# A transformer block with a SwiGLU feed-forward: gate, up and down each as seven block products, in two phases

## The reference

```
D_MODEL = 2048; SEQ = 512; D_FF = 5632
def swiglu(h, wg, wu, wd):
    return (jax.nn.silu(h @ wg) * (h @ wu)) @ wd
...
h = rms_norm(x, norm_ffn_g[i])
x = x + swiglu(h, ffn_w_gate[i], ffn_w_up[i], ffn_w_down[i])
```

## Time and profile before

| | us |
|---|---|
| median of three runs | 2318.69 |
| lowest and highest of them | 2315.89, 2318.73 |
| the profiled execution | 2316.0 |
| its span, first to last instruction | 2314.1 |
| TensorE busy in it | 2288.2 (99%) |
| VectorE busy | 1305.3 (56%) |
| ScalarE busy | 777.7 (34%) |
| mean granted TensorE clock | 0.995 |

### The profile page before, as it was taken

The page is one execution under the profiler, slowest core; times in us unless marked ns, Lnnn a source line. Parts: engine busy times, 40 slices in busy tenths (PEclk is TensorE's granted clock), DMA queues, the critical chain, the costliest instruction groups (busy, mean ns, idle before and its releaser), DMA issues.

```text
span 2314.1 us, 30956 instructions
## 1 busy us (share of the span) xinstructions
PE 2288.2 (99%) x11963; PEld 1967.9 (85%) x11963; DVE 1305.3 (56%) x1993; ACT 777.7 (34%) x1163; POOL 76.2 (3%) x89
## 2 busy tenths in 40 slices
PE   8999999999999999999999999999999999999998
PEld 7898989889889999888888888888888888888886
DVE  5333466665765556456464646465565646464647
ACT  4332344443453334222332323232332323232322
POOL 1000000000010000000000000000000000000000
PEclk9999999999999999999999999999999999999999
DMA  5343211222123213355253544435343535253434
GB/s 162 115 118 87 79 52 50 65 64 64 56 82 111 74 59 97 95 168 147 92 154 92 155 119 125 140 109 150 115 137 110 145 99 151 91 151 119 128 109 137
DMA packets 225456, 252.81 MB, mean 109 GB/s; under 512 B 14172, under 2 KB 188273, under 8 KB 224161
## 3 DMA queue, kind: packets, MB, share of 16 engines
q1 hardware_dynamic: 218050, 222.36, 30.5%
q0 software_dynamic: 7264, 28.51, 6.4%
HBM read 223.55 MB, written 4.19 MB: 98 GB/s over the span
## 4 chain that ended last, share of the span: by engine, by line
PE 77%; issue 19%; DVE 2%; POOL 1%; ACT 1%; DMA 0%; POOLq 0%; SPq 0%; ACTq 0%; DVEq 0%
PE ps L1266 76%; POOL rqn L415 1%; DVE wl L759 0%; PE ps L1577 0%; DVE hTl L759 0%; DVE x_rows L773 0%; PE ps L1613 0%; PE ps L1313 0%; DVE x_rows L1187 0%; POOL krr L415 0%; DMA down<-in_ffn_w_down_dram 0%; DVE down L1162 0%; ACT wh L455 0%; ACT hTh L455 0%; ACT x_sq L472 0%
## 5 line engine op out<-in xcount | busy, mean ns | idle before, releaser
L1266 PE MATMUL ps<-hTh,wh 128*128 128x512 f32 (+1 forms) x1968 | 764.0, 388 | 2.4 <-DVE wl L759 1.8
L1266 PE MATMUL ps<-hTh,wl 128*128 128x512 f32 (+1 forms) x1968 | 760.1, 386 | 0.0
L1266 PE MATMUL ps<-hTl,wh 128*128 128x512 f32 (+1 forms) x1968 | 759.7, 386 | 0.0
L759 DVE TENSOR_TENSOR wl<-raw,wh 128x1024 fp32r<-128x1024 f32 x298 | 363.3, 1222 | 341.8 <-ACT wh L455 339.1
L455 ACT ACTIVATE wh<-raw 128x1024 fp32r<-128x1024 f32 x298 | 314.2, 1058 | 534.6 <-PE ps L1266 416.7
L1266 PEld LDWEIGHTS ps<-hTh,wh 128*128 128x128 f32 x1968 | 370.0, 188 | 75.2 <-issue 2.2
L1266 PEld LDWEIGHTS ps<-hTh,wl 128*128 128x128 f32 x1968 | 369.8, 188 | 75.1
L1266 PEld LDWEIGHTS ps<-hTl,wh 128*128 128x128 f32 x1968 | 370.0, 188 | 72.2
L759 DVE TENSOR_TENSOR wl<-down,wh 128x1024 fp32r<-128x1024 f32 x132 | 161.4, 1223 | 157.0 <-ACT wh L455 157.0
L1266 PE MATMUL ps<-wh,opsh 128*128 128x512 f32 x616 | 240.9, 391 | 6.1 <-DVE x_rows L1187 4.4
L1266 PE MATMUL ps<-wl,opsh 128*128 128x512 f32 x616 | 240.4, 390 | 0.0
(11 more groups left out here) (181 smaller groups left out, 2014.2 us busy)
## 6 DMA issues: line engine op xcount, KB each, us to landing
raw<-in_ffn_w_gate_dram SPq DMA_DIRECT2D x176, 256.0 KB, 3.0
raw<-in_ffn_w_up_dram SPq DMA_DIRECT2D x176, 256.0 KB, 3.0
down<-in_ffn_w_down_dram SPq DMA_DIRECT2D x176, 256.0 KB, 3.2
raw<-in_nsa_w_in_dram SPq DMA_DIRECT2D x164, 256.0 KB, 3.0
raw<-in_nsa_w_out_dram SPq DMA_DIRECT2D x64, 256.0 KB, 3.0
t<-in_ffn_w_down_dram SPq DMA_DIRECT2D x44, 256.0 KB, 3.3
down<-down POOLq DMA_DIRECT2D x22, 512.0 KB, 6.1
t<-down POOLq DMA_DIRECT2D x22, 512.0 KB, 6.0
```

What stands on the lines that cost most here:

```text
L759: nc.vector.tensor_tensor(dst, src, hi.bitcast(f32), ALU.subtract).then_inc(done, 1)
L1266: return nc.tensor.matmul(out_, a, b, start=start, stop=stop, skip_group_check=True)
```

## The change

The feed-forward no longer mixes gate/up with down. It has two phases of in all 19 *turns*, each made of seven products of U units (12 matmuls of 128x512 each, activations stationary):

- Turns 0 to 10, one for each slab, U = 4, so 28 units: gate and up together form one product of [512 tokens x 2048] with [2048 x (512 gate + 512 up)], as a 2x2 block scheme (tokens in halves, the 2048 rows in halves, gate against up) with seven products.
- Turns 11 to 18, the down product. The hidden rows are taken in four chunks of 3, 3, 3 and 2 slabs, and each chunk has two turns, one for each half of the 2048 output columns. U = 3 in turns 11 to 16 (21 units), U = 2 in turns 17 and 18 (14 units).

The units run product by product: position pos = j*U + u holds product j (0 to 6) of unit u. The scheme needs seven left operands. For turns 0 to 10 they are formed once, in turn 0 and just before it, from the transposed rows: ScalarE copies quarters out of PSUM with the gain (`left_evacuate`), VectorE makes 16 sums and differences (`left_combine_a`, `_b`, `_c`), and both split them (`left_high`, `left_low`). They take the memory of `hTh`, `hTl` and others, so x2 is spilled to DRAM (`x2_dram`) and read back in turn 11. At the end of an up turn results are combined on VectorE (lines of `w_at`, `c22_at`, `v_at`, `c21`, `c12`), pass through silu (`gate`) and `product`, are transposed by TensorE (`m_tiles`, 2 x 8 transposes at positions 4 and 8 of the following turn), combined (`m_combine`) and stored to DRAM (`store_m`, eight transfers a slab). In the down phase the left operands are read back one by one (`form_load`, 256 KB each, 77 in all), and split by ScalarE (128x512) and VectorE (128x512).

Of each turn's four weight sums, VectorE makes the first (`sum_a`, one unit ahead) and the third (`sum_c`); the second and fourth are adding transfers on GpSimd's queue into `g1`. The high ring keeps four units, the low ring has three.

```diff
-UPS = [("g", j) for j in range(G_UNITS)]
-MIXED = [("g", 0), ("g", 1), ("d", 0), ("d", 1)] \
...
+CHUNKS = [(0, 3), (3, 6), (6, 9), (9, SLABS)]
+DOWN0 = SLABS
+TURNS = DOWN0 + 2 * len(CHUNKS)
+PRODUCTS = 7
+HI_RING, LO_RING = 4, 3
...
+def forming():
...
+                if c == 0:
+                    where = (t - 1, 25 + k // 2 * 2) if k < 3 else (t, k - 3)
+                elif U == 3:
+                    where = (t - 1, max(10 + k // 2, k + 3)) if k < 12 else (t, 10 + (k - 12) // 2)
...
+            def form_load(c, j, u, f):
...
+                else:
+                    sp.wait_ge(form_lo, f - STAGES + 1)
+                sp.wait_ge(m_stored, 128 * (s + 1))
+                sp.dma_start(formed[f % STAGES][:, :, :], m_dram[s][:, j, :, :]).then_inc(form_loaded[f % STAGES], 16)
...
+            for t in range(TURNS):
+                U = units_of(t)
+                for pos in range(PRODUCTS * U):
...
+                    if t == DOWN0 and pos == 1:
+                        sp.wait_ge(lo_ready, unit_end(DOWN0 - 1, 6))
+                        sp.dma_start(x_rows[:, 0:2, :], x2_dram[:, 0:2, :]).then_inc(y_loaded, 16)
...
+                    u = pos - 6 * U
+                    if 0 <= u < units_of(t + 1):
+                        if t == DOWN0 - 1:
+                            sp.wait_ge(units_used, unit_end(t, 6))
+                        sp.wait_ge(lo_ready, unit_at(t, 6, u) + 1)
+                        weights(t + 1, 1, 1, u, g2(t + 1)[u], loaded2[u])
...
+            for t in range(TURNS):
+                U, sums = units_of(t), units_before(t)
+                for u in range(U):
+                    pool.wait_ge(loaded1[u], 32 * (t + 1))
+                    pool.wait_ge(loaded2[u], 32 * (t + 1))
+                    pool.wait_ge(ta_done, sums + u + 1)
+                    pool.dma_start(g1[u][:, :], g2(t)[u][:, :], accum_op=ALU.add).then_inc(tb_done[u], 16)
+                for u in range(U):
+                    pool.wait_ge(loaded0[u], 64 * (t + 1))
+                    pool.wait_ge(lo_ready, unit_at(t, 3, u) + 1)
+                    pool.dma_start(g1[u][:, :], g0[u][:, :], accum_op=ALU.add).then_inc(td_done[u], 16)
...
+                q1_at, s5_at, s7_at, s56_at = (14, 12, 18, 19) if up else (7, 9, 12, 15) if U == 3 else (5, 7, 9, 11)
...
+            def sum_a(t, u):
+
+                n = unit_at(t, 1, u)
+                dve.wait_ge(units_used, n - LO_RING + 1)
...
+            def sum_c(t, u):
+
+                dve.wait_ge(tb_done[u], 16 * (t + 1))
+                dve.wait_ge(lo_ready, unit_at(t, 2, u) + 1)
+                nc.vector.tensor_tensor(g1[u][:, :], g1[u][:, :], g0[u][:, :], ALU.add).then_inc(tc_done, 1)
...
+                    if 1 <= t <= DOWN0 and pos in (4, 8):
+                        m_tiles(t, pos // 4 - 1)
...
+                    if u == 0 and j == 3:
+                        pe.wait_ge(s5_copied, t + 1)
```

More of the change, by code:

```diff
@@ new lines, in nsa_swiglu_block @@
+        g2_down = [over(f"g3_{u}", [P, UNIT], q_at + 36 * KB + 4 * KB * u) for u in range(3)]
+        works_up = [over(f"work{i}", [P, 2, S], x_at + (16 + 4 * i) * KB) for i in range(4)]
+        works_down = [over(f"dwork{i}", [P, 2, S], a) for i, a in enumerate(
+            (q_at + 48 * KB, q_at + 52 * KB, k_at, k_at + 4 * KB))]
+        formed = [over(f"formed{i}", [P, 2, 256], a) for i, a in enumerate(
+            (spare_at[1], spare_at[1] + 2 * KB, h_at + 60 * KB, h_at + 62 * KB))]
+        x2_dram = nc.dram_tensor("x2_scratch", [S, D], f32, kind="Internal").ap().rearrange("(t p) d -> p t d", p=P)
@@ L366, in _ @@
[L366 to L375, removed]
@@ new lines, in _ @@
+            for u in range(4):
+                if u < 2:
+                    sp.wait_ge(lo_ready, F0 - 1 + u)
+                else:
+                    sp.wait_ge(units_used, F0 - 2)
+                weights(0, 0, 0, u, g0[u], loaded0[u])
+            sp.wait_ge(units_used, F0)
+            for u in range(4):
+                weights(0, 0, 1, u, g1[u], loaded1[u])
+            sp.wait_ge(x2_spilled, 64)
+            sp.wait_ge(x2_sq, 16)
+            sp.wait_ge(h2T_banks, 16)
+            for u in range(4):
+                weights(0, 1, 1, u, g2_up[u], loaded2[u])
@@ L381, in _ @@
+            out_v = out[0].rearrange("(t p) d -> p t d", p=P)
+            for n in range(2):
+                done = TURNS - DOWN0 - 1 + n
+                for added, row, b in ((y22_added, 2, 1), (y11_added, 0, 0), (y21_added, 2, 0), (y12_added, 0, 1)):
+                    at = (slice(None), slice(row, row + 2), slice(n * 1024 + b * 512, n * 1024 + b * 512 + 512))
+                    sp.wait_ge(added, done)
                     sp.dma_start(out_v[at], x2[at]).then_inc(stored, 16)
@@ new lines, in _, with gate @@
+            for c in range(4):
+                for n in (B0 + 2 * c + RING, B0 + 2 * c + 1 + RING):
+                    if n < F0:
+                        split(n)
+                if c:
+                    left_evacuate(c - 1)
+                    left_high(0, c - 1)
+                squares(c)
+            high(0, 0, 0)
+            high(0, 0, 1)
+            left_evacuate(3)
+            left_high(0, 3)
+            high(0, 0, 2)
+            def gate(t, half, tile):
+                dst = works_up[1 if half else 3][:, tile, :]
+                src = dst if half else pair(pairs_of(t)[0])[:, tile, :]
+                nc.scalar.activation(dst, src, ACT.Silu, scale=rr[:, 2 * half + tile:2 * half + tile + 1])\
+                    .then_inc(gate1_done if half else gate0_done, 1)
@@ L1252, in _ @@
[L1252 to L1260 removed]
+            nc.vector.tensor_scalar(rr[:, :], rr[:, :], 1.0 / D, EPS, ALU.mult, ALU.add).then_inc(rms_den, 1)
@@ L1652, in product @@
-            def product(n, j):
-                o, b = LEFT[j % QUAD], down_bank(j)
-                for tt in range(2):
-                    for kk in range(2):
-                        ts, at = slice(tt * P, (tt + 1) * P), slice(kk * 512, (kk + 1) * 512)
-                        last = mm3(bank(b + tt), (opsh[:, kk, o, ts], opsl[:, kk, o, ts]),
-                                   (wh[:, n % RING, at], wl[:, n % RING, at]), kk == 0 and j % QUAD in (0, 1, 3), kk == 1)
-                last.then_inc(units_used, 1)
```

802 lines of the change are left out of this document (490 added, 312 removed).

## The result

| | before | after |
|---|---|---|
| median of the runs, us | 2318.56 | 2300.90 |
| lowest and highest | 2315.89, 2318.73 | 2297.99, 2303.71 |
| the profiled execution, its span | 2316.0, 2314.1 | 2301.4, 2299.6 |

The changed kernel takes 0.9926 of the time (95% interval 0.9909 to 0.9944): 17.7 us less, where 57 had been forecast (54.7 by the sum). The sign was right, the size was a third.

The account below looks back on a forecast made before the run. TensorE's matmul pace was taken as the bound, busy 99% of the span. Savings of 119.7 and 9.5 us less added costs summed to -54.7: 2316.0 to 2261.3, stated as 2262 us, own range 2246 to 2290, stated range 2238 to 2302.

Parts of the forecast that it names:

- (c): Start of turn 0: TensorE waits for copies, combinations and splits of the first operands; +15.3 us (12 to 22).
- (a): Transposes of the products, 22 times 8 at 0.9 us; +19.8 us.
- (b): Position 4 of 11 turns: TensorE waits for VectorE's `m0_done`, 0.73 us a turn; +8.0 us (0 to 12).
- (d): Change of phase into turn 11: SP's blocked queue delays form loads, first matmul at T + 7.4; +14 us (8 to 28).
- (e): Three-unit turns: form loads wait for one of four buffers, 1 us a turn, five turns; +5 us (0 to 30).
- (f): Two two-unit turns: position 6 waits for a copy behind splits and sums after an adding transfer; +11.2 us (6 to 20).
- (g): The end: two additions in place of one behind the last matmul; +1.2 us.
- What it removes: Feed-forward: 528 fewer matmuls at the same pace, -119.7 us; the 9.5 us around the last slab's hand-over, -9.5.
- three-unit turns of more than 60 us: Sign in the down phase that the forecast is wrong and the transfer engines bound; forecast had a 57.1 us turn.
- The rival of the transfer engines: Down phase: transfer engines bound, each round loses 3 us, 6 us more a turn over six: 2298 us; chance 0.17.
- The rule weighed there: Skill's rule for GpSimd transfers: 3.2 us for 512 KB, so (f) would vanish and the sum be 2250; trace preferred.
- Additions late in every turn: Adding transfers, 132 for 44, land later than before; at 16 us landing 2335 us; chance 0.09.

Follow-up runs that it names:

- vector_second: Against after, the second adding transfer of each unit in turns 12 to 18 replaced by a VectorE addition: 2267.37 us.
- no_second_add: Against after, the second adding transfer of each unit left out from turn 12 on, with ScalarE's waits for them: 2267.70 us.
- copy_and_tiles: Against after, ScalarE's copy of product 1 at position 5 in two-unit turns, the first eight transposes at position 5 in turns 1 to 11: 2293.12 us.
- second_round: Against after: second sum on VectorE, opened boundary, copy and transposes moved, turn 11's stores and x2 loads rearranged, forms still two a position: 2238.55 us.
- one_form: Against after, forms of the second to fourth chunk made one at a position from position 3 of the turn before: 2280.85 us.

## Why the forecast was wrong, step by step

| term | forecast | measured in after |
|---|---|---|
| attention and projections, not touched | 0 | +3.7 |
| (c) start of turn 0 | 15.3 | 14.2 |
| (a), (b) an up turn, turns 1 to 10 | 78.7 each | 78.9 each |
| (d) turn 11, with its wait of (b) | 14.7 | 26.8 |
| (e) turns 12 to 16 | 5 | 30.1 |
| (f) last two turns | 11.2 | 6.6 |
| (g) tail, added to 4.6 | 1.2 | 4.1 |

**What it removes** held: 528 matmuls less at the same pace, and the old hand-over gone. **(a), (b), (c)** held to a microsecond or two; TensorE waits 0.66 to 0.69 us a turn for the last product (0.69 in the row at 1029.34), and the start of turn 0 has the two waits foreseen. The 3.7 us ahead of the feed-forward are scatter: the last matmul before the transposes starts between 920.4 and 925.3 us in the eleven profiles of after and its variants.

**(e) is the step that failed**, 30.1 us for 5. The formula was right and its input was wrong. A round is 0.2 + 0.44 + landing + 0.6 + 0.6 for 5.44 us of matmuls. The prediction bounded the landing by 3.0 and 6.6, said in the same breath that the engines would be fuller, and then took the lower end, 1 us a turn. With the median of 6.1 a round is 7.9, 2.5 too long, and in the burst it is longer still: the pairs of form loads issued at 1910.98, 1913.26, 1916.38 and 1920.89 land after 4.0, 6.2, 9.5 and 7.8 us (the first of each), and the buffer of the third pair takes its next load only at 1927.31, 10.9 us later. The lead of the splits pays some of that; 3.5 to 4.5 us reach TensorE, and with the restart a turn is 5.3 to 7.2 us longer. With 4.0, as in vector_second, a round is 5.8, and the 0.4 too much vanishes in the lead. So somewhere between median landings of 4.0 and 6.1 the loss goes from 0.2 us a turn to 6.0; no run shows where. The prediction had named three-unit turns of more than 60 us as the sign of the transfer engines, and they took 62.4 to 64.3.

Why the landing is 6.1 was in the rows too. The rival of the transfer engines counted 79% of a three-unit turn and "6 us more a turn"; the share was 69%, and the loss 6.0 a turn, and its 2298 us lie 3 from the measured time. It lost as a forecast because "the loads of weights run four units ahead" was held against it. They do, and it does not matter: it is not the weights that are late but the one small load without a lead. And the mean share was the wrong number to look at; within the 10 us of the burst it was 1.04. The Trainium skill, DMA: Bandwidth & Descriptors, section Issuing engines are not separate DMA queues, says that transfers started by any engine run on the same 16 and interleave; the trace agrees, since taking away 19 transfers of GpSimd's queue brought SP's form loads from 6.1 to 4.0 us in the median.

**(d)** failed in its second half. The first wait came as worked out (8.2 us idle for a start at T + 7.4, measured T + 8.3), the load behind x2's first half landed at T + 17.1 (T + 17), and TensorE reached position 4 12.5 us late (13). That the last two agree is in part luck: 2.5 us of it are a half-speed restart that the sum had not, and position 3 (1.0 us idle) waited for VectorE's queue, not for that load; the transposes at position 4 waited 1.8. What the sum lacked is later. At position 13 SP stands at the store of the last slab with a form load behind it, and the engines are full at the same time (4.15 us idle, 7.1 with the restart, for which the sum had nothing); near the end x2 stands in VectorE's way (3.36 idle, 5.2 in all, for which it had 2). Both are waits for something that is queued ahead.

**(f)**: right in mechanism, TensorE waits at position 6 for ScalarE's copy `dwork`, 2.84 and 2.09 us idle, and no_second_add, where they stay, and copy_and_tiles, where they go, show that it is the place of the copy. It was too large by 4.6: 2.8 of that is the half-speed restart that did not come, the rest the wait, which cost 3.0 and 2.3 us for 4.2, less some small losses elsewhere. The rule weighed there, 3.2 us for an adding transfer (the Trainium skill, DMA: Bandwidth & Descriptors, section Anatomy of one DMA), is contradicted by every run: the medians lie between 5.1 and 5.8 us, and between 4.5 and 7.2 in the stretch 1890 to 2190, with the engines 58% to 72% busy.

**(g)** was an omission. In the last turn an adding transfer needs 9.43 us and puts VectorE behind for the rest of it; the chain of waits of after shows the landing and the last of the additions queued behind the end of TensorE at 2290.91:

```profile
2270.77 9.43 DMA g<-g
...
2282.20 0.95 ACT wh L590
...
2292.50 1.23 DVE x_rows L1463
2293.72 1.15 DVE dwork L1447
...
2294.89 1.23 DVE x_rows L1463
```

Without that transfer the tail is 5.9 us, which is the 4.6 + 1.2 of the sum.

*Additions late in every turn* fell: the landing is 5.8 in the median, and up turns never wait for a sum. Single landings did pass the 9 us that the prediction had named as a sign of it (9.15 in turn 12, 9.43 in turn 18).

In figures: 37.2 us of the miss are (d) and (e), 3.7 scatter, 2.9 the tail, 2 the up turns, less 4.6 of (f) and 1.1 of (c): 40.1, and the profiled executions stand at 2261.3 forecast and 2301.4 measured. What stays open is how much of the last waits of turn 11 in second_round is the adding transfers there and how much the stores' place; no kernel here takes the adding transfers out of turn 11.

## What to carry to other kernels

Find the transfer that has the least lead, write its round as a sum, and price it at the landing that holds at that very moment: lay the bursts of *all* queues on one time axis, since the share of an average hides a full 10 us. Where a small load goes round through few buffers, the cheapest cures are to spread its uses, or to take another queue's transfers off that moment, even at the price of an instruction on a busier engine: 19 additions of 1.22 us on VectorE, 65% busy, bought 33 us. And a queue that stands at a wait holds back everything written behind it, however small (8.2 us here for one load of 256 KB).

## What the runs showed of the hardware

- An adding transfer from SBUF to SBUF takes 5.2 us of all 16 engines a MB, a load from DRAM 3.0, and it lands after 4.6 us with the engines 61% busy, 6.5 with 69%.
- A load of 256 KB (a left operand) lands after 4.0 or 6.1 us in the same two cases; single ones took 10.9 us in turn 12 of after and 10.53 in second_round, where the DMA share was 1.05.
- How TensorE restarts does not follow from the idle time alone. In turn 12, after 3.72 us, matmuls ran at 0.23 for 1.5 us and only then at 0.427, at half the clock (1.2 of 2.4 GHz; the granted clock is 1.00 from 1931.7 to 1933.2 and 0.50 from there to 1936.6). In turn 11, after 4.15 us, the granted clock is 0.50 from the restart at 1862.65 on. After 2.84 us none was slow, where one_form has eight intervals of 0.43 after 2.07 us (restart at 2247.07) and the kernel before slowed down after 2.40. First turn 12, then turn 17:

```profile
1933.00 0.44 PE L1547 MATMUL ps<-wh,down_lo 128*128 128x512 f32 x1
1933.24 0.63 PE L1547 MATMUL ps<-wh,down_hi 128*128 128x512 f32 x1
1933.66 0.63 PE L1547 MATMUL ps<-wl,down_hi 128*128 128x512 f32 x1
...
2228.05 0.40 PE L1547 MATMUL ps<-wl,down_hi 128*128 128x512 f32 x1
2228.28 0.39 PE L1547 MATMUL ps<-wh,down_lo 128*128 128x512 f32 x1
```
